# Each down product behind its own up product in the 64-place groups, and another order of the weight loads

## The reference

```python
x = x + merged @ w_out                                   # mixers, not touched
h2 = rmsnorm(x, g_ffn)
idx, wts = route(h2, w_router, router_bias)              # top 8 of 64 experts
moe = routed_experts(h2, idx, wts, w_exp_gate, w_exp_up, w_exp_down) + swiglu(h2, shared weights)
x = x + moe
x = x + sigmoid(rmsnorm(x, g_ple) @ w_ple_gate) * rmsnorm(p @ w_ple_proj, g_ple_post)
```

## Time and profile before

| | us |
|---|---|
| median of three runs | 1023.71 |
| the profiled execution | 1023.04 |
| its span, first to last instruction | 1020.8 |
| TensorE busy in the span | 952.3 |
| transfers of in-weights, of the chain that ended last | 19% of the span |

### The profile page before, as it was taken

How to read it: one execution, slowest core, us unless ns; L and a number is a source line. 1 busy time by engine, 2 the same in 40 slices (tenths; PEclk the granted TensorE clock), 3 DMA queues, 4 the chain that set the end, 5 groups by cost and what they waited for, 6 DMA issues and landing times.

```text
span 1020.8 us, 14891 instructions
## 1 busy us (share of the span) xinstructions
PE 952.3 (93%) x6015; PEld 418.7 (41%) x6015; DVE 297.5 (29%) x707; ACT 166.2 (16%) x308; POOL 167.7 (16%) x319
## 2 busy tenths in 40 slices
PE   6999999999999999999999999989969998984698
PEld 4554544444445543443333333345323333331244
DVE  3322552002224743333332111111101111110677
ACT  2002221122001121111111111111111112111021
POOL 4236000000000012222222222212121212111010
PEclk9999999999999999999999999999989999998799
DMA  9441211210191589999999999999999999996982
GB/s 336 138 146 61 83 42 42 82 67 17 40 344 42 204 316 347 417 409 412 405 412 405 411 418 401 394 416 414 397 422 421 421 421 421 418 403 256 376 298 83
DMA packets 82148, 294.90 MB, mean 289 GB/s; under 512 B 9148, under 2 KB 35680, under 8 KB 57888
## 3 DMA queue, kind: packets, MB, share of 16 engines
q1 hardware_dynamic: 67472, 255.90, 63.8%
q0 software_dynamic: 11920, 33.86, 8.5%
q10 hardware_dynamic: 2688, 4.19, 1.1%
HBM read 277.14 MB, written 25.17 MB: 296 GB/s over the span
## 4 chain that ended last, share of the span: by engine, by line
PE 72%; DMA 23%; DVE 2%; SPq 1%; issue 1%; ACT 0%; POOL 0%; POOLq 0%; DVEq 0%; ACTq 0%
PE ps L1904 21%; DMA ring<-in_w_exp_up 19%; PE ps L1556 11%; PE ps L1933 7%; PE ps L1659 5%; PE ps L2030 4%; PE ps L1540 3%; PE ps L1500 3%; PE ps L1643 3%; PE ps L1641 3%; PE ps L1477 2%; DMA ring<-accumulator 2%; DMA ring<-in_w_exp_down 1%; PE ps L1730 1%; PE ps L1506 1%; SPq L450 1%
## 5 line engine op out<-in xcount | busy, mean ns | idle before, releaser
L1904 PE MATMUL ps<-ring,gates 128*32 128x512 f32 x2560 | 288.5, 603 | 28.4 <-DMA ring<-in_w_exp_up 27.7
L1904 PEld LDWEIGHTS ps<-ring,gates 128*32 128x32 f32 x2560 | 88.1, 111 | 220.9 <-issue 220.0
L1933 PE MATMUL ps<-ring,poolbuf 128*32 128x512 f32 x1280 | 145.6, 595 | 3.0 <-DMA ring<-in_w_exp_down 3.0
L1318 DVE COPY poolbuf<-ps 128x256 f32<-128x256 f32 x40 | 17.0, 425 | 357.6 <-PE ps L1913 357.6
L1556 PE MATMUL ps<-actT,ring 128*128 128x512 f32 x256 | 112.3, 595 | 0.0
L661 POOL TENSOR_TENSOR tickets<-cst 128x1 f32<-128x1 f32 x77 | 14.6, 189 | 398.2 <-ACT actT L850 392.7
L1556 PEld LDWEIGHTS ps<-actT,ring 128*128 128x128 f32 x256 | 47.9, 190 | 59.6 <-issue 59.5
L1933 PEld LDWEIGHTS ps<-ring,poolbuf 128*32 128x32 f32 x1280 | 37.9, 109 | 83.4 <-issue 81.7
L850 ACT ACTIVATE actT<-ps,qT 128x1024 f32<-128x1024 f32 x40 | 44.6, 1114 | 142.2 <-PE ps L1933 142.2
L842 ACT ACTIVATE poolbuf<-ps 128x256 f32<-128x256 f32 x40 | 15.4, 385 | 281.6 <-PE ps L1904 281.6
L2030 PE MATMUL ps<-ring,actT 128*128 128x512 f32 (+1 forms) x144 | 59.8, 568 | 0.5 <-DVE actT L1434 0.5
(11 more groups left out here) (242 smaller groups left out, 870.8 us busy)
## 6 DMA issues: line engine op xcount, KB each, us to landing
ring<-in_w_exp_down SPq DMA_DIRECT2D x64, 1024.0 KB, 17.4
ring<-in_w_exp_gate SPq DMA_DIRECT2D x62, 1024.0 KB
ring<-in_w_exp_up SPq DMA_DIRECT2D x62, 1024.0 KB
ring<-accumulator SPq DMA_DIRECT2D x12, 1024.0 KB, 13.8
ring<-in_w_gate SPq DMA_DIRECT2D x8, 1024.0 KB, 13.6
ring<-in_w_in SPq DMA_DIRECT2D x5, 1024.0 KB
ring<-in_w_out SPq DMA_DIRECT2D x4, 1024.0 KB
ring<-in_w_ple_gate SPq DMA_DIRECT2D x4, 1024.0 KB
```

The source lines that it names most:

```text
L1904: last = mm(bank(2 + k)[part, :], hgT[k][:, q, part], pair_view(EXPERT_SLOT[js[c]])[:, q], start=(q == 0), stop=(q == KD - 1))
L1933: last = mm(bank(6 + half)[part, :], eactT[r % 2][:, q, part], w[:, q, half * 512:(half + 1) * 512], start=(q == 0), stop=(q == 1))
```

## The change

From step 25 (`OWN_AT`) on, the down product of a step runs in that step: TensorE's order becomes up(r), rows_T(r+1), the job of slot 0, acts_T(r), down(r), the job of slot 1. At step 25 acts_T(24) and down(24) run first, before up(25). ScalarE and VectorE follow with `weigh(r)` and `act_T(r)`. Nothing is left behind step 39.

SP's order for the 64-place groups becomes: down weights of experts 2 and 3 of g-1, in-weights of experts 0 and 1 of g, down weights of experts 0 and 1 of g, in-weights of experts 2 and 3 of g. For g = 9 the first two stay in their old order.

```diff
--- before.py
+++ after.py
@@ -52,6 +52,7 @@
 STEP_OF = [(g, s) for g in range(NGROUP) for s in range(GROUP * (CAP if g < BIG_GROUPS else CAP2) // P)]
 STEPS = len(STEP_OF)
 FIRST_STEP = [STEP_OF.index((g, 0)) for g in range(NGROUP)]
+OWN_AT = FIRST_STEP[BIG_GROUPS] + 1
 TCOL, WCOL = 2, 4
 LCOL = TCOL + 2 * WCOL
 LATE = (2, 3)
@@ -518,6 +519,10 @@
                 pos, step = g * GROUP, FIRST_STEP[g - 1]
                 e = [sp.value_load(order[0:1, pos + j:pos + j + 1], min_val=0, max_val=NE - 1)
                      for j in range(GROUP)] if g < NGROUP else None
+                if late and g - 1 > BIG_GROUPS:
+                    down_used(step - 1)
+                    load_down(pos - 2, late[0])
+                    load_down(pos - 1, late[1])
                 if e:
                     in_used(step)
                     load_in(pos, e[0])
@@ -525,7 +530,7 @@
                         load_ple_proj()
                     if g - 1 >= BIG_GROUPS:
                         load_in(pos + 1, e[1])
-                if late:
+                if late and g - 1 <= BIG_GROUPS:
                     down_used(step - 1)
                     load_down(pos - 2, late[0])
                     load_down(pos - 1, late[1])
@@ -540,6 +545,9 @@
                     down_used(step + 1)
                     load_down(pos + 1, e[1])
                 elif e:
+                    down_used(step)
+                    load_down(pos, e[0])
+                    load_down(pos + 1, e[1])
                     in_used(step + 1)
                     if step == SMALL_AT + 2:
                         load_shared_down()
@@ -548,9 +556,6 @@
                     else:
                         load_in(pos + 2, e[2])
                         load_in(pos + 3, e[3])
-                    down_used(step)
-                    load_down(pos, e[0])
-                    load_down(pos + 1, e[1])
                 return e and e[2:]
 
             late = None
@@ -875,11 +880,12 @@
                     rows_hi(r + 1, (r + 1) % 2)
                 for n in jobs_of(r, 0):
                     job(n)
-                if r:
+                if 0 < r <= OWN_AT:
                     weigh(r - 1)
+                if r >= OWN_AT:
+                    weigh(r)
                 for n in jobs_of(r, 1):
                     job(n)
-            weigh(STEPS - 1)
 
             def o_start(j):
                 all_scattered(act)
@@ -1343,8 +1349,20 @@
                 nc.vector.tensor_tensor(pp[:, i, half * 512:(half + 1) * 512], bank(5),
                                         gpost[:, half * 512:(half + 1) * 512], ALU.mult).then_inc(ple_copied, 1)
 
+            def job(n):
+                if n < 6 and n % 3 < 2:
+                    late_T(n // 3, n % 3)
+                elif n < 6:
+                    shared_mult(LATE[n // 3])
+                elif n < 8:
+                    shared_T(n - 6)
+                elif n < 8 + 2 * NT:
+                    base(n - 8)
+                else:
+                    ple_gain(n - 8 - 2 * NT)
+
             for r in range(STEPS):
-                if r:
+                if 0 < r <= OWN_AT:
                     act_T(r - 1, (r - 1) % 2)
                 act_rows(r, r % 2)
                 if r + 1 < STEPS:
@@ -1357,18 +1375,12 @@
                     weights_of(r, found_of(r))
                     if r + 1 < NGROUP:
                         places(r + 1, rank3[:, :, (r + 1) * GROUP:(r + 2) * GROUP])
-                for n in jobs_of(r, 0) + jobs_of(r, 1):
-                    if n < 6 and n % 3 < 2:
-                        late_T(n // 3, n % 3)
-                    elif n < 6:
-                        shared_mult(LATE[n // 3])
-                    elif n < 8:
-                        shared_T(n - 6)
-                    elif n < 8 + 2 * NT:
-                        base(n - 8)
-                    else:
-                        ple_gain(n - 8 - 2 * NT)
-            act_T(STEPS - 1, (STEPS - 1) % 2)
+                for n in jobs_of(r, 0):
+                    job(n)
+                if r >= OWN_AT:
+                    act_T(r, r % 2)
+                for n in jobs_of(r, 1):
+                    job(n)
 
 
             nc.vector.tensor_copy(o_iota, cst[:, C_IOTA + 1:C_IOTA + CAP + 1]).then_inc(o_iota_ready, 1)
@@ -1950,8 +1962,11 @@
             rows_T(0)
             shared_up(1, 4, 8)
             for r in range(STEPS):
+                if r == OWN_AT:
+                    acts_T(r - 1)
+                    down(r - 1)
                 up(r)
-                if r:
+                if 0 < r < OWN_AT:
                     acts_T(r - 1)
                 if r + 1 < STEPS:
                     rows_T(r + 1)
@@ -1959,12 +1974,13 @@
                     lists(r)
                 for n in jobs_of(r, 0):
                     job(n)
-                if r:
+                if 0 < r < OWN_AT:
                     down(r - 1)
+                if r >= OWN_AT:
+                    acts_T(r)
+                    down(r)
                 for n in jobs_of(r, 1):
                     job(n)
-            acts_T(STEPS - 1)
-            down(STEPS - 1)
 
 
             def o_start(j):
```

## The result

| | before | after |
|---|---|---|
| median of 14 runs each, us | 1023.47 | 1026.41 |
| the profiled execution, us | 1023.04 | 1027.08 |
| its span, us | 1020.8 | 1024.6 |
| share of TensorE in the chain that ended last | 72% | 82% |
| share of DMA in it | 23% | 13% |

The ratio of the runs is 1.0029, with a 95% interval of 1.0019 to 1.004: 2.9 us slower. The forecast was 1024.4, 0.9 above the median now measured for before; the change cost 2 us more than that. The time lies inside the range, which is 7 us wide because it was made for the rivals too. The interval leaves out a ratio of 1, so the kernel is a little slower; the difference is just under the 3.1 us that the prediction took as what can be told from no change.

What follows compares the result with a forecast made beforehand. The prediction took the expert stage to be bound by one long stream of weight transfers. Its sum was 1023.04 + 0 + 0 + 0 + 0.7 = 1023.7, 1024.4 us on the median's scale, range 1021.3 to 1028.3.

Steps and rivals of the forecast that it cites:

- Part 1: SP's load order: up products from group 10 about 5 us later, last landing stays at 928.4, nothing blocks; 0 us.
- Part 3: Start of the new order, steps 24 to 27: up(27) ends at 731.5, queue lasts until 736.0; 0 us.
- rival (a): Transfer queue runs dry at step 27 (+4 us), or TensorE bounds steps 34 to 37 (+3.2); 1027.6 to 1028.4; chance 0.19.
- Part 2: Down behind its own up: tightest step, with projection job, 17.2 us against 17.35 of stream, so covered; 0 us.
- Part 4: End of the expert stage: last down product starts at 928.4 to 929.5, 0 to +1.1 us, taken as +0.7.
- Rival (b): Fuller DMA engines remove slow stretches, 2.1 us at the end and 2.0 around step 27; 1021.0; chance 0.13.
- Rival (c): Products wait for their own down weights, but hidden under up's 7.07 us; forecast's time, counted in its 0.68 chance.

Runs made afterwards that it cites:

- e10: Kernel before the change, with the scatter of step 37 held back until down(38) is done; 1022.24 us, ratio 0.9986.
- e11: The same kernel as e10, run once more; 1023.17 us, ratio 0.9991.
- a1: The changed kernel, unedited, run again for a second profile; 1026.72 us, ratio 1.0034.
- e12: The changed kernel with the scatters of steps 37 and 38 held back until up(39) is done; 1027.29 us, ratio 1.0048.
- e1: The changed kernel, but from step 25 on acts_T and VectorE's copy stand before the job of slot 0; 1026.5 us, ratio 1.0025.
- e9: e1 with the scatters of steps 37 and 38 held back until up(39) is done; 1024.71 us, ratio 1.0018.
- e6: e1, but the last group (steps 38 and 39) keeps the old order of products and loads; 1024.07 us, ratio 1.0011.
- e4: Kernel before the change with SP's new load order alone, products in the old order; 1045.38 us, ratio 1.0214.
- e8: e1 with the scatter of step 38 held back until up(39) is done; 1027.55 us, ratio 1.0042.
- e2: The changed kernel, but both halves of the change begin at group 10 (step 29) instead of group 8 (step 25); 1026.23 us, ratio 1.0032.
- e3: The changed kernel with the edits of e1 and e2 together; 1025.91 us, ratio 1.0024.
- e5: Kernel before the change with the new product order alone, SP's loads in the old order; 1042.14 us, ratio 1.0171.

## Why the prediction was right or wrong

Right in kind and within its range, and low by 2 us. The picture behind the number held only in part: I had the stream as the bound up to up(39), each up product behind a wait for in-weights, and in the changed kernel up(35) to up(39) wait for none.

To place the cost, here are distances within one execution each, in us from the start of up(24), which no kernel changes (starts of PE's rows; MB is the length times GB/s of the window up to up(34)):

| profile | up(34) | MB moved by then | up(38) | last down product |
|---|---|---|---|---|
| before | 172.44 | 71.6 | 241.86 | 269.27 |
| e10, before, scatter held | 171.74 | 72.0 | 241.14 | 267.26 |
| e11, the same | 172.75 | 72.4 | 241.83 | 271.09 |
| changed | 179.68 | 74.7 | 249.48 | 271.56 |
| a1, the same | 179.80 | 74.6 | 249.60 | 271.67 |
| e12, changed, scatters held | 180.37 | 74.7 | 250.07 | 272.15 |
| e1, acts first | 180.53 | 74.9 | 248.19 | 272.05 |
| e9, acts first, scatters held | 180.46 | 74.5 | 248.44 | 270.69 |
| e6, last group old | 180.37 | 74.9 | 248.45 | 270.60 |

**Part 1, the load order.** Right that nothing blocks: SP's waits did not hold each other up, and e4 shows what it looks like when they do. But its size was short. I had every up product 5.05 us later, the price of one pair of down weights. In the table up(34) is 7.2 to 8.1 us later than before, and up(38) still 6.3 to 6.6 later where TensorE is off the bound (e1, e6, e9). Of the three profiles that the table leaves out, e8 agrees with e1 (180.56 and 248.20), e2 has up(34) at 179.17 and e3 up(38) at 247.25, 6.7 and 5.4 us later than before. That e1 and e9 have up(38) at 906.84 and 905.71 us, close to my 906.1, is luck: their up(24) began 0.5 and 1.9 us earlier than in the profile of before. No time was lost in the stream, whose windows up to up(34) have 415 and 416 GB/s. More lay ahead: about 3 MB more had moved by up(34), where a pair is 2.1. The rest is one scatter and one gather: GpSimd issues 11 scatters and 10 gathers between up(24) and up(34) before, and 12 and 11 in the changed kernel, because each down product, and with it the scatter and the gather behind that, now comes a step earlier. A scatter or gather is about 0.42 MB (33.86 MB in 80 of them on the page, an estimate), so the sum is 2.9 MB. I had priced the pair alone, though I had the scatter's 1.1 us in hand. This is the first term that was too small, by 1.3 to 1.5 us at up(38).

**Part 3, the transition.** Right, closely: down(24) at 677.91 (forecast 677.8), up(27) ending at 731.2 (731.5), SP's issue at 731.37, no bytes lost from 640 to 760 us, and e2 recovered nothing. The first branch of rival (a), a queue that runs dry there, is refuted. The clock cost 1.3 us in down(24), of the 2 us that I had allowed, and nothing in up(25) behind it (7.05 us). The rule of the Trainium skill that I cited against the change ("TensorE: Matmul & The Clock Gate", section "HAM oscillation — how this bites in real kernels"), by which a wait for DMA brings the array back to half clock, agrees with the trace here: the granted clock is 0.72 from 675 to 680 us.

**Part 2, the step with a projection job.** This step failed. I had 17.2 us against 17.35 of stream (my terms add up to 17.27, so the slack was 0.08 us and not 0.15); the runs show 17.41 to 17.50. rows_T takes 1.00 us in front of the job, not 0.88 (864.03 to 865.03), and from the job's start to the down product are 4.01 us, not 3.85 (3.92 in steps 36 and 37). That is the second branch of rival (a), by a tenth of a us a step. What I had not seen at all is that the weights come closer together at the end of the stage: in e1 up(37) and up(38) follow at 16.9 and 16.1 us (873.86, 890.75, 906.84), not at 17.35. The stream is no faster there, 416 GB/s from 890.75 to 906.84 as before the change from 883.67 to 901.03; it has less to carry. Before, the last gather of rows goes out between up(37) and up(38), in e1 a step earlier. First before, then e1:

```profile
884.25 1.05 POOL L673 DMA_INDIRECT rows<-h_rows,stage  x1 [0.51 <-issue]
```

```profile
874.64 1.05 POOL L678 DMA_INDIRECT rows<-h_rows,stage  x1 [0.51 <-issue]
```

A TensorE with no slack can't follow, and up(38) came 2.1 us later, counted from up(34), than in e1. Counted from up(24) the difference is 1.3 us.

**Part 4, the end.** Its chain was nearly right: 22.08 us from up(38) to the last down product, against 22.3 to 23.4 in my working, weights included. But from that late up(38) it ends at 931.42, not at 928.4 to 929.5. And the stream would not have allowed much better. I had the second half of the last in-weights at 922.3 to 923.4; in e1 and e8 it came at 924.59 and 924.98 us, 17.8 to 17.9 us behind up(38) instead of 16.2. I had moved the scatter of step 38 in front of weights in my sum, not that of step 37, which the change also moves: it went out at 915.16 before, 2 us ahead of the landing of the last half, and at 906.80 in e1, 18 us ahead of it. e9 and e10 agree with that price of 1.1 us and more. Against it: e11 shows 17.75 us without that scatter, and before the change the scatter of step 36 went out at 899.52 us, in nearly the same place (1.5 us ahead of up(38)), and the half came at 16.2. Whether the scatter is the cause stays open.

**Where the 2.9 us are, then.** By the table the changed kernel reaches up(38) 7.6 us later than before, not 5.05, and its chain from there is 22.08 us against 27.41, where 22.36 would have kept the time: +2.3 us in all at the last down product, and +2.4 in the second profile. These are single executions, and the two of one kernel in e10 and e11 lie 3.8 us apart in the last column, though only 0.7 to 1.0 us in the others. So the lateness of up(34) and up(38) is well shown, and the last column supports the sum only roughly. Two bounds lie side by side at the end: TensorE's unbroken chain (the changed kernel, twice, and e12) and the late weights behind it (e1, e3). Removing the first leaves 1.0025, easing the second alone in e12 brings nothing, both together give 1.0018 (e9), and giving up the new order in the last group 1.0011 (e6). What is left in e9 and e6 fits Part 1: up(38) still comes 6.6 us later, not 5.05 (by my prices a pair and a scatter are 6.15), and the last down product 1.3 to 1.4 us later than before (270.60 and 270.69 against 269.27). Behind the last down product, a part of spread has nothing to do with the change: from the moment all scatters are in (GpSimd's memset) to the end of the span it took 83.3 us in the profile of before, 84.1 and 85.5 in the two of the changed kernel, and 85.3 in e10, which has the old order. Much of the difference lies in the first products of the last gate, which run at a low clock for longer or shorter (4.75 us before, 5.82 and 6.27 in the two of the changed kernel for the same eight instructions, at granted clocks of 0.76, 0.62 and 0.57).

**Rival (b)**, a gain from fuller engines: the last stretch did move more, 400 GB/s against 388 from 901 to 928.4 us, and nothing came of it. Its price was worked out wrongly too: 2.1 and 2.0 us off the forecast of 1024.4 give 1020.3, not 1021.0. **Rival (c)**, waiting for own down weights, appears in the changed kernel only at down(24), as forecast; e5 is what it would be without the load order.

## What to carry to other kernels

When a stage is bound by a stream of transfers, count every byte that the change moves ahead of a landing, the gathers and stores of the steps included: one pair of weights was priced, 3 MB had moved. Price each step of the engine behind the stream against the stream's lightest stretch, not its mean: 0.1 us of slack in a sum with four hand-overs is none, and when the stream had less to carry at the end, the engine stayed behind. And a queue order and a product order belong together: each half alone cost 17 to 22 us, the pair 3. The fastest version found is the kernel before with one scatter held back (0.9986 and 0.9991), and the second interval does not exclude no change.

## What the runs showed that I had not expected

- SP can be held in issuing itself. With many transfers under way the issue of the last in-weight half took 5.71 us in the changed kernel (902.75 us) and 6.20 in e1, against 0.33 to 0.41 for those just before in the changed kernel. The kernel before is held too, by about 2 us in each of its last three half issues. So the last down weights, whose slots were free at 907.4 in the changed kernel, went out only from 908.6 us on, 4.5 us earlier than the 913.1 of before. First after, then before:

```profile
902.75 5.71 SPq L465 DMA_DIRECT2D ring<-in_w_exp_up  x1
908.55 2.40 SPq L470 DMA_DIRECT2D ring<-in_w_exp_down  x2
```

```profile
898.17 2.10 SPq L464 DMA_DIRECT2D ring<-in_w_exp_up  x1
```

- The bytes moved by 640 us, where all these kernels still do the same, differ by 1 MB between the two profiles of the changed kernel (153.4 and 154.3, summed over windows) and by 1.8 over all (152.7 in e3, 154.5 in e9), which is 2.3 and 4.4 us of the stream at 0.41 MB a us. That is as much as the effect looked for, or more.
